# Gated one-hot rows of four tokens made together, tokens innermost, in a fused attention, recurrence and expert kernel

## What is computed

```python
idx = jnp.take_along_axis(cand_i, best_pos, axis=-1)      # i1 * 128 + i2, 128 picks a token
gates = jax.nn.softmax(best_s, axis=-1)
h = gelu(einsum('chkd,cd->chk', peer_u[idx], x)) * gates
out = einsum('chk,chkd->cd', h, peer_v[idx])
```

## Time and profile before

| | before |
|---|---|
| median of 3 runs | 990.09 us (989.94 to 995.99) |
| the profiled execution | 990.32 us |
| its span | 988.5 us |
| PE busy | 974.9 us (99%) |
| DVE, ACT, POOL busy | 745.3, 627.9, 598.4 us |
| granted TensorE clock | 0.998 of full |

### The profile page before, as it was taken

How to read it: one execution, slowest core, us unless ns; L and a number is a source line. 1 busy time by engine, 2 the same in 40 slices (tenths; PEclk the granted TensorE clock), 3 DMA queues, 4 the chain that set the end, 5 groups by cost and what they waited for, 6 DMA issues and landing times.

```text
span 988.5 us, 22607 instructions
## 1 busy us (share of the span) xinstructions
PE 974.9 (99%) x7344; PEld 917.9 (93%) x7344; DVE 745.3 (75%) x1718; ACT 627.9 (64%) x1232; POOL 598.4 (61%) x292
## 2 busy tenths in 40 slices
PE   8999999999999999999999999999999999999997
PEld 7998899999899999989999999989999999999996
DVE  7684663544747798878788888879888878888886
ACT  6874375556557666666888888865555555555553
POOL 3685624687318999989877777874433334444420
PEclk9999999999999999999999999999999999999999
DMA  7473313455545666656555555599888887988871
GB/s 258 141 243 120 125 40 105 128 188 200 205 154 172 211 212 204 205 187 212 174 187 171 176 174 174 174 333 392 317 318 313 308 312 277 336 313 310 314 277 43
DMA packets 61821, 215.05 MB, mean 218 GB/s; under 512 B 7203, under 2 KB 9251, under 8 KB 61644
## 3 DMA queue, kind: packets, MB, share of 16 engines
q1 hardware_dynamic: 51980, 180.04, 53.2%
q0 software_dynamic: 9216, 33.56, 9.1%
q10 hardware_dynamic: 576, 0.82, 0.2%
HBM read 212.89 MB, written 1.06 MB: 216 GB/s over the span
## 4 chain that ended last, share of the span: by engine, by line
PE 93%; DVE 3%; POOL 2%; ACT 1%; DMA 1%; issue 0%; ACTq 0%; DVEq 0%; POOLq 0%
PE PS L988 21%; PE PS L922 19%; PE PS L993 11%; PE PS L926 10%; PE PS L493 4%; PE PS L494 4%; PE PS L495 4%; PE PS L871 3%; PE PS L503 2%; PE PS L879 2%; PE PS L948 1%; POOL lo L1505 1%; PE PS L949 1%; PE PS L657 1%; PE PS L507 1%; PE PS L912 1%
## 5 line engine op out<-in xcount | busy, mean ns | idle before, releaser
L1505 POOL TENSOR_TENSOR lo<-raw,hi 128x1024 fp32r<-128x1024 f32 x191 | 459.6, 2413 | 156.0 <-ACT hi L1069 141.6
L1069 ACT CAST hi<-raw 128x1024 fp32r<-128x1024 f32 x203 | 212.5, 1048 | 41.7 <-DMA raw<-in_u_units 15.3
L922 PE MATMUL PS<-xb,hi 128*128 128x448 f32 x1024 | 235.0, 371 | 2.2 <-ACT arena L1356 2.2
L988 PE MATMUL PS<-xb,hi 128*128 128x448 f32 x1008 | 228.7, 368 | 0.0
L922 PEld LDWEIGHTS PS<-xb,hi 128*128 128x128 f32 x1024 | 183.0, 189 | 14.6 <-issue 2.4
L988 PEld LDWEIGHTS PS<-xb,hi 128*128 128x128 f32 x1008 | 179.9, 189 | 11.8
L2172 DVE TENSOR_TENSOR lo<-raw,hi 128x1024 fp32r<-128x1024 f32 x126 | 153.9, 1222 | 24.2 <-ACT hi L1402 24.2
L1439 ACT CAST xb<-arena 128x224 fp32r (+1 forms) x126 | 47.9, 380 | 143.2 <-PE PS L993 143.2
L926 PEld LDWEIGHTS PS<-xb,lo 128*128 128x128 f32 x1024 | 133.7, 191 | 4.7 <-POOL lo L1505 0.7
L993 PEld LDWEIGHTS PS<-xb,lo 128*128 128x128 f32 x1008 | 132.7, 191 | 4.1
L1402 ACT CAST hi<-raw 128x1024 fp32r<-128x1024 f32 x128 | 133.9, 1046 | 3.9 <-DMA raw<-in_v_units 3.9
(11 more groups left out here) (353 smaller groups left out, 1518.4 us busy)
## 6 DMA issues: line engine op xcount, KB each, us to landing
raw<-in_u_units SPq DMA_DIRECT2D x128, 512.0 KB, 3.3
raw<-in_v_units SPq DMA_DIRECT2D x128, 512.0 KB, 4.4
raw<-in_w_in_units SPq DMA_DIRECT2D x43, 512.0 KB, 3.3
raw<-in_w_q_units SPq DMA_DIRECT2D x16, 512.0 KB, 3.4
raw<-in_w_proj_units SPq DMA_DIRECT2D x8, 512.0 KB, 4.3
raw<-in_w_out_units SPq DMA_DIRECT2D x8, 512.0 KB, 4.3
arena<-bias_rows SPq DMA_DIRECT2D x2, 512.0 KB, 4.8
arena<-in_subkeys_t SPq DMA_DIRECT2D x1, 1024.0 KB, 6.3
```

The costliest lines, as they stand in the source:

```text
L922: mm(o[:, 0:2 * TD].rearrange("p (s t) -> p s t", s=2), hi[:, w, P * k:P * k + P], xb[:, k, :, 0:TD], start=(k == 0), stop=False, skip_gro ...
L988: return mm(PS[:, V_BANKS[c], 0:2 * TD].rearrange("p (s t) -> p s t", s=2), hi[:, (U_V + j) % 4, P * c:P * c + P], coef_slot(u + j)[:, :, ...
L1069: nc.scalar.copy(hi[:, j, :], raw[:, j, :]).then_inc(hi_made, 1)
L1505: nc.gpsimd.tensor_tensor(lo[:, w, :], raw[:, w, :], hi[:, w, :].bitcast(F32), ALU.subtract).then_inc(lo_pool, 1)
```

## The change

`oh1` gets the layout of `oh2`: 128 columns by four tokens, tokens innermost. It is made by a comparison over 512 columns and, after a wait for it, a multiplication in place by the 16-bit gates of four tokens, which is broadcast over the 128 columns. The comparison for `oh2` stands between the two. The four `tensor_scalar` instructions go. `hot_made` now counts 2 per unit. PE's streamed operand for the high part, and ACT's input for the low part, are read four elements (8 bytes) apart; `oh1_low` stays contiguous.

In the setup, `i2T` becomes `i2_half` in 16 bit, `gT` and the single row of numbers go, and the 16-bit gates are copied to PSUM (`high_ps`).

```diff
-        oh1 = nc.alloc_sbuf_tensor_at("oh1_high", [P, 2, 4, P], F16, offset=hot_at)
+        oh1 = nc.alloc_sbuf_tensor_at("oh1_high", [P, 2, P, 4], F16, offset=hot_at)
+        i2_half = nc.alloc_sbuf_tensor_at("i2_half", [P, T], F16, offset=early_at + 4 * T)
-        rows_half = PS[:, 7, P:P + P // 2]
+        high_ps = PS[:, 6, 0:P]
@@ gated_unit, PE
-                pe.wait_ge(hot_made, n + 1)
+                pe.wait_ge(hot_made, 2 * n + 2)
-                    mm(o, oh2[:, j % 2, :, k], oh1[:, j % 2, k, :], start=True, stop=False)
+                    mm(o, oh2[:, j % 2, :, k], oh1[:, j % 2, :, k], start=True, stop=False)
@@ low_one_hots, ACT
-                act.wait_ge(hot_made, n + 1)
+                act.wait_ge(hot_made, 2 * n + 2)
-                    last = nc.scalar.activation(oh1_low[:, j % 2, k, :], oh1[:, j % 2, k, :], ACT.Copy,
+                    last = nc.scalar.activation(oh1_low[:, j % 2, k, :], oh1[:, j % 2, :, k], ACT.Copy,
@@ setup, DVE
-            V.tensor_copy(i2T[:], PS[:, 3, 0:T]).then_inc(picks_sb, 1)
-            V.tensor_copy(gT[:], scaled_ps).then_inc(picks_sb, 1)
-            link(V.tensor_copy(g_high[:], scaled_ps))
+            V.tensor_copy(i2_half[:], PS[:, 3, 0:T]).then_inc(picks_sb, 1)
+            V.tensor_copy(g_high[:], scaled_ps).then_inc(picks_sb, 1)
+            dve.wait_ge(picks_sb, 3)
-            V.tensor_copy(oh1[:, 0, 0, :], iota_ps)
-            V.tensor_copy(rows_half, oh1[:, 0, 0, :].bitcast(F32))
+            V.tensor_copy(high_ps, g_high[:].bitcast(F32))
@@ one_hots, DVE
-                for k in range(4):
-                    t = 16 * i + (4 * j + k)
-                    V.tensor_scalar(oh1[:, j % 2, k, :], rows_half.bitcast(F16), i2T[:, bass.ds(t, 1)], gT[:, bass.ds(t, 1)],
-                                    ALU.is_equal, ALU.mult)
-                V.tensor_tensor(oh2[:, j % 2], rows4_half.bitcast(F16).rearrange("p (a b) -> p a b", b=4),
-                                i1_half[:, bass.ds(16 * i + 4 * j, 4)].unsqueeze(1).to_broadcast([P, P, 4]),
-                                ALU.is_equal).then_inc(hot_made, 1)
+                rows = rows4_half.bitcast(F16).rearrange("p (a b) -> p a b", b=4)
+
+                def four(a):
+                    return a[:, bass.ds(16 * i + 4 * j, 4)].unsqueeze(1).to_broadcast([P, P, 4])
+                V.tensor_tensor(oh1[:, j % 2], rows, four(i2_half), ALU.is_equal).then_inc(hot_made, 1)
+                V.tensor_tensor(oh2[:, j % 2], rows, four(i1_half), ALU.is_equal)
+                dve.wait_ge(hot_made, 8 * i + (2 * j + 1))
+                V.tensor_tensor(oh1[:, j % 2], oh1[:, j % 2], four(high_ps.bitcast(F16)), ALU.mult).then_inc(hot_made, 1)
```

More of the change, by code:

```diff
@@ L2065, in _ @@
             V.tensor_copy(i1_half[:], PS[:, 2, 0:T]).then_inc(picks_sb, 1)
-            V.tensor_copy(i2T[:], PS[:, 3, 0:T]).then_inc(picks_sb, 1)
-            V.tensor_copy(gT[:], scaled_ps).then_inc(picks_sb, 1)
-            link(V.tensor_copy(g_high[:], scaled_ps))
+            V.tensor_copy(i2_half[:], PS[:, 3, 0:T]).then_inc(picks_sb, 1)
+            V.tensor_copy(g_high[:], scaled_ps).then_inc(picks_sb, 1)
+            dve.wait_ge(picks_sb, 3)
             link(V.tensor_tensor(scaled_ps, scaled_ps, g_high[:], ALU.subtract))
             ratio = PS[:, 6, 0:T]
-            dve.wait_ge(picks_sb, 3)
             link(V.tensor_scalar(ratio, g_high[:], 1e-30, None, ALU.max))
```

## The result

The changed kernel takes 1003.19 us (median of 4 runs, 1002.26 to 1004.09) against 990.13 us before (median of the three runs given above and a fourth, 990.18). The ratio is 1.0123, with a 95% interval of 1.0107 to 1.0139: slower by about 13 us. The forecast was no change, 990.1 us, with a range that ended at 996.

The account below looks back on a forecast made before the run. The prediction took PE to bound the kernel, busy for 145.91 of 146.00 us in the gated stage. Terms of 0 from DVE, ACT, PE and setup left 990.3, or 990.1 us by the runs' median; range 987 to 996.

Parts of the forecast that it names:

- DVE's saving: DVE's one-hots per gated unit: 1.08 us instead of 1.43, 0.35 us less, all becoming idle time, so 0 on the total.
- the lower bound: DVE's multiplication for `oh1`: 0.42 us from below, as L2090 takes, against 0.69 from above; 0.42 was chosen.
- The setup: One-time copies before the stage: DVE through about half a microsecond earlier, PE not waiting for it, effect 0.
- the wait for `hot_made`: PE's wait in each gated unit: one more register operation, costing 0 because PE's queue runs ahead.
- Rival B: ACT's four L1394 per unit become the bound by their strided read: up to 995.5 us, chance 0.04.
- Rival C: A gain from 0.10 us of slack before PE's first gated load: at most 5.6 us, 984.5 us, chance 0.04.
- the term of PE: Four high-part matmuls per gated unit, streaming `oh1` 8 bytes apart: 0 taken, from bounds of 0 and 12.3 us.
- Rival A: The four L948 per unit fetch their streamed operand slower: 991 to 996 us, or 1002.4 at the upper bound; chance 0.15.
- the trace agrees for the weights: PE's eight weight loads per gated unit already read `oh2` 8 bytes apart and fit within the 0.056 us pitch.

## Why the prediction was wrong

**What held.** That PE bounds the stage, that DVE's saving ends as idle time, and its size: 1.07 us for the one-hots where 1.08 was forecast, the product at the lower bound, 0.41 us. The 61.1 us of the 224 L2088 became 23.2 + 23.0 = 46.2 us. The setup and the wait for `hot_made` cost nothing. Rival B was right in that ACT pays, but by 0.009 us an instruction, 0.398 instead of 0.389 (page of the profile, L1395), far from the 0.083 at which it would matter. Rival C, a gain from the 0.10 us before the first gated load, did not come: in the run with contiguous streams the stage took 168.5 us, 168.3 before.

**The step that failed** is the term of PE, in the sentence "I take 0, by the nearest row, the weights". The right place was named and both bounds were written down, 0 and 12.3 us; the measured 12.8 us of the stage lies just over the upper one. The pitch by which the bound was made, 0.111 us for 128 columns in 32 bit, is close to the 0.118 us of the stepped stream, but no run shows that the two are the same thing, so that the upper bound came out so near is in part luck. What failed is the choice between them: weights were called nearest because they were at the same step in the same matmul. The runs show that a step costs them differently: at a step of 8, 0.17 us more for a stream and under 0.01 for weights. Rival A had the right place, the right cause (the step of the stream) and a price near the measured one (1002.4 against 1003.2). Its reason, the bytes over which the 128 columns are spread, holds only in part: a matmul took 0.06 us at 256 and at 512 bytes, 0.12 at 1024, 0.23 at 2048, and still 0.23 at 4096. Its chance of 0.15, 0.09 of it for about the bound, was low for a term without a row, and the range, which left it out, should have held it: the one uncovered term of the sum had two bounds and no row of its own kind.

The Trainium skill, Advanced Engine Details and Errata, section Memory Cachelines, has two hits on a 16-byte line as enough to hide its cost. The trace does not agree for a stream of 16 bit: two hits a line took 0.118 us where four or eight took 0.056. The size of the line agrees with the steps of 8 and 16 costing the same. Nor does the trace quite bear out the prediction's "the trace agrees for the weights", as it had no contiguous load to compare with: stepped loads were 0.118 us long where contiguous ones took 0.097, though before the change the pitch of 0.056 us did not show it.

## What to carry to other kernels

Where PE is the bound, look at what a new layout does to the operand that it streams before counting what it saves elsewhere: in these runs a matmul of 128 columns of 16 bit cost nothing more at a step of 4 bytes, twice as much at 8, and four times at 16 and at 32. If one engine wants tokens innermost and another contiguous rows, let the engine with idle time read with the step and write in order, not the other way round. When a term without cover has one bound at zero and the other at 12 us, and the row that speaks for zero is of another path, the range has to hold both.

## What the runs showed of the hardware that was not expected

- A stepped weight load is nearly free: at a step of 16 bytes it was 0.144 us long instead of 0.113 at a step of 8, and cost under 0.01 us of pitch; a stream at the same 16 bytes takes 0.23 us instead of 0.056.
- A DVE product of 512 columns in 16 bit takes 0.41 us with everything in order, 0.677 us when it reads 8 bytes apart (and its gates are repeated along the columns), and 2.51 us when it writes 256 bytes apart. With 128 columns written 8 bytes apart `tensor_scalar` takes 0.551 us instead of 0.334.
- One transfer that comes late costs more than the wait. ACT waited 2.39 us for it, PE stood still for 1.39 us, then its granted clock was 0.50, the lower of its two levels (1.2 instead of 2.4 GHz), for some 3 us, and 3.5 us were lost in all.
